# Two hybrid layers on one core: the second linear-attention pair moved behind the four softmax heads

## What is computed

```python
h = rms_norm(x, norm_g[l]) * (1.0 + scale) + shift
gq, gk, gv, glr, gz, dq, dk, dv, dz = split_columns(h @ w_in[l])
gq, gk, gv = split(silu(causal_depthwise_conv(concat(gq, gk, gv), conv_w[l])))
# gla, 4 heads: log_a = log_sigmoid(glr @ w_gk + b_gk) / 16, b = cumsum over chunks of 64
# k_dec = k * exp(b_end - b); state = exp(b_end) * state + k_dec^T v; o = q @ state
# o = rms_norm(o, g_out) * silu(z)
# diff, 4 heads: q, k rms-normed, p = softmax of the masked scores of two halves,
# o = rms_norm((p0 - lam * p1) @ v, g_out) * (1 - lam_init) * silu(z)
x = x + gate * (concat(o_gla, o_diff) @ w_out[l])
```

## Time and profile before

| | |
|---|---|
| median of 3 runs | 1952.38 us (1950.65 to 1952.73) |
| the profiled execution's own time | 1950.45 us |
| its span, first to last instruction | 1948.6 us |
| TensorE busy | 1849.8 us, 95% of the span |
| VectorE, ScalarE, GpSimd busy | 1017.4, 879.6, 876.4 us |
| layers of the second model | about 1361 to 1658 us and 1658 to 1948 us |

### The profile page before, as it was taken

The page is one execution under the profiler, slowest core; times in us unless marked ns, Lnnn a source line. Parts: engine busy times, 40 slices in busy tenths (PEclk is TensorE's granted clock), DMA queues, the critical chain, the costliest instruction groups (busy, mean ns, idle before and its releaser), DMA issues.

```text
span 1948.6 us, 26470 instructions
## 1 busy us (share of the span) xinstructions
PE 1849.8 (95%) x8630; PEld 1448.3 (74%) x8630; DVE 1017.4 (52%) x1675; ACT 879.6 (45%) x1371; POOL 876.4 (45%) x1064
## 2 busy tenths in 40 slices
PE   7999989999999999999899999999899989899988
PEld 5666657887888788888788787888677757676756
DVE  5667646611653468677566315623534454634451
ACT  6667644411432355555444213423445544535551
POOL 3322245655666334434236656765443325443323
PEclk9999999999999999999899999999999999999999
DMA  4121115433443221212145324523222112222212
GB/s 153 55 66 54 54 55 162 162 97 108 162 140 97 87 76 55 65 54 66 33 136 173 117 93 151 166 93 97 67 74 66 65 44 76 69 83 63 68 44 76
DMA packets 49659, 176.37 MB, mean 91 GB/s; under 512 B 5648, under 2 KB 5776, under 8 KB 49568
## 3 DMA queue, kind: packets, MB, share of 16 engines
q1 hardware_dynamic: 42368, 148.99, 24.2%
q10 hardware_dynamic: 7200, 26.22, 4.0%
HBM read 173.08 MB, written 2.10 MB: 90 GB/s over the span
## 4 chain that ended last, share of the span: by engine, by line
PE 79%; DVE 8%; ACT 7%; issue 4%; POOL 1%; DMA 0%; DVEq 0%; ACTq 0%; SPq 0%; POOLq 0%
PE ps_g L236 22%; PE ps_g L240 21%; PE ps_g L243 21%; PE ps_zt L938 2%; PE ps_s L1501 1%; PE ps_o L966 1%; PE ps_zt L1556 1%; ACT w_hi L208 1%; PE ps_o L494 1%; PE ps_o L1571 1%; PE ps_zt L484 1%; ACT scr L393 1%; PE ps_s L385 1%; DVE scr L1124 1%; PE ps_zt L476 1%
## 5 line engine op out<-in xcount | busy, mean ns | idle before, releaser
L216 POOL TENSOR_TENSOR w_lo<-raw,w_hi 128x256 fp32r<-128x256 f32 x936 | 764.7, 847 | 880.1 <-ACT w_hi L208 879.4
L208 ACT ACTIVATE w_hi<-raw 128x1024 fp32r<-128x1024 f32 x274 | 288.9, 1054 | 375.5 <-PE ps_g L243 361.6
L236 PE MATMUL ps_g<-h_hi,w_hi 128*128 128x512 f32 x1240 | 349.7, 412 | 22.2 <-ACT h_hi L270 8.5
L240 PE MATMUL ps_g<-h_lo,w_hi 128*128 128x512 f32 x1240 | 326.3, 393 | 1.0 <-DVE h_lo L275 1.0
L243 PE MATMUL ps_g<-h_hi,w_lo 128*128 128x512 f32 x1240 | 323.3, 391 | 0.3 <-DVE w_lo L224 0.3
L236 PEld LDWEIGHTS ps_g<-h_hi,w_hi 128*128 128x128 f32 x1240 | 225.6, 190 | 91.5 <-issue 39.8
L240 PEld LDWEIGHTS ps_g<-h_lo,w_hi 128*128 128x128 f32 x1240 | 234.9, 189 | 53.8 <-DVE h_lo L275 2.3
L243 PEld LDWEIGHTS ps_g<-h_hi,w_lo 128*128 128x128 f32 x1240 | 234.0, 189 | 50.9 <-DVE w_lo L224 0.7
L236 PE MATMUL ps_g<-a_hi,w_hi 128*128 128x512 f32 x920 | 249.3, 405 | 18.2 <-DVE scr L1730 4.5
L240 PE MATMUL ps_g<-a_lo,w_hi 128*128 128x512 f32 x920 | 238.5, 394 | 0.0
L243 PE MATMUL ps_g<-a_hi,w_lo 128*128 128x512 f32 x920 | 237.3, 392 | 0.0
(11 more groups left out here) (197 smaller groups left out, 2056.6 us busy)
## 6 DMA issues: line engine op xcount, KB each, us to landing
raw<-weights SPq DMA_DIRECT2D x274, 512.0 KB, 3.5
scr<-ada_weights ACTq DMA_DIRECT2D x48, 512.0 KB, 4.3
x<-x_tiles SPq DMA_DIRECT2D x8, 256.0 KB, 5.4
y<-x SPq DMA_DIRECT2D x8, 256.0 KB, 3.2
scr<-csil_dram ACTq DMA_DIRECT2D x2, 512.0 KB, 5.5
lvmask<-level_masks SPq DMA_DIRECT2D x1, 512.0 KB, 8.5
mats<-squares SPq DMA_DIRECT2D x1, 448.0 KB, 6.6
vecs<-vectors SPq DMA_DIRECT2D x1, 95.5 KB, 2.0
```

What stands on the lines that cost most here:

```text
L208: nc.scalar.activation(w_hi[:, t.rep % 2], raw[:, raw_slot(t)], ACT.Copy).then_inc(whi_ready, 1)
L216: ins = nc.gpsimd.tensor_tensor(w_lo[:, t.rep % 2, ks], raw[:, raw_slot(t), ks], w_hi[:, t.rep % 2, ks].bitcast(F32), ALU.subtract)
L236: nc.tensor.matmul(bank[:], w_hi[:, t.rep % 2, kk], rhs(k)[0], start=(first and n == 0), stop=False)
L240: nc.tensor.matmul(bank[:], w_hi[:, t.rep % 2, kk], rhs(k)[1], start=False, stop=False)
```

## The change

Two things, in both layers. **The gates' order**: `gate 0`, `gate 1` go ahead of the first half of tile 4, and what follows from them (`gate2`, `decay`, the silu table, `silu 0`) comes one or two half tiles earlier. **The items' order**: g0, d0, d1, d2, d3, g1. The second pair's six tiles are now numbers 23 to 28. Its convolutions start while d3's softmax is still going on, and its six silus come in three stretches, each between two loads of tables (two more loads a stretch). The drain holds g1's `read` and two `stat` steps in place of d3's softmax, so d3 loses its own banks and waits as the other heads do. Output row blocks are taken in the order 0, 1, 4, 5, 6, 7, 2, 3 (`BLOCK`), as their heads finish. `dec_b`, `ktok_b`, `vtok_b` get a buffer for each pair.

```diff
-B2_COLUMNS = [GLA_Z, GLA_Z + P, GLA_R]
...
+B2_COLUMNS = [GLA_Z, GLA_Z + P, GLA_R, GLA_Q, GLA_K, GLA_V, GLA_V + P]
 for _h in range(DIFF_HEADS):
     B2_COLUMNS += [m + P * _h for m in (DIFF_Q, DIFF_K, DIFF_V, DIFF_Z)]
+B2_COLUMNS += [GLA_Q + P, GLA_K + P, GLA_V + 2 * P, GLA_V + 3 * P, GLA_Z + 2 * P, GLA_Z + 3 * P]
...
-        ITEMS = [("gla", p) for p in range(GLA_PAIRS)] + [("diff", h) for h in range(DIFF_HEADS)]
+        ITEMS = [("gla", 0)] + [("diff", h) for h in range(DIFF_HEADS)] + [("gla", 1)]
...
+        OWN["gla1"] = {2 * c + 1: [("taps", c)] for c in range(4)}
+        OWN["gla1"][5][:0] = [("functions", SILU), ("silu", 0), ("silu", 1), ("functions", EXP_LN)]
+        OWN["gla1"][8] = [("functions", SILU), ("silu", 2), ("silu", 3), ("functions", EXP_LN)]
+        OWN["gla1"][10] = [("functions", SILU), ("silu", 4)]
+        OWN["gla1"][11] = [("silu", 5), ("functions", EXP_LN)]
+        for _i, _s in ((2, "decay"), (6, "decay2")):
+            OWN["gla1"].setdefault(_i, []).append((_s,))
+        for _i, _t in ((7, "k"), (9, 0), (10, 1)):
+            OWN["gla1"].setdefault(_i, []).append(("turn", _t))
+        OWN["gla1"][11].append(("update",))
...
+        DRAIN = [("split",), ("out", 0, 0, 6), ("read", G1), ("square", 0, G1), ("out", 1, 0, 2), ("stat", 0, G1),
+                 ("square", 1, G1), ("out", 1, 2, 6), ("olo", 0, G1), ("stat", 1, G1), ("out", 0, 6, 7), ("out", 1, 6, 7),
+                 ("olo", 1, G1)]
...
-                        due[2] += [("gate", p) for p in range(GLA_PAIRS)]
-                        due[3].append(("gate2", 0))
-                        due[4] += [("gate2", 1), ("decay", it)]
-                        due[5].insert(0, ("functions", SILU))
+                        due[1] += [("gate", p) for p in range(GLA_PAIRS)]
+                        due[2] += [("gate2", 0), ("gate2", 1)]
+                        due[3] += [("decay", it), ("functions", SILU, it), ("silu", 0, it)]
                         due[7].append(("decay2", it))
...
+        BLOCK = [0, 1, 4, 5, 6, 7, 2, 3]
```

More of the change, by code:

```diff
@@ L225, in split_lo_dve, with gemm @@
                                     ALU.subtract).then_inc(wlo_ready, 1)
-        def gemm(pe, t, o, rhs, kts, first, last, waits=None, free=None):
+        def gemm(pe, t, o, rhs, kts, first, last, waits=None, free=None, used=None):
             pe.wait_ge(whi_ready, t.of(1, 1))
@@ L244, in gemm @@
                                        stop=(last and n == len(kts) - 1))
-            if kts[-1][1] == KT - 1:
+            if kts[-1][1] == KT - 1 if used is None else used:
                 ins.then_inc(tile_used, 1)
@@ L1254, in hg_pool @@
                 if a: hg_d_pool(pool, a, l)
-        ITEMS = [("gla", p) for p in range(GLA_PAIRS)] + [("diff", h) for h in range(DIFF_HEADS)]
-        FIRST_TILE = {it: 3 + 4 * it[1] if it[0] == "gla" else 1 + 6 * GLA_PAIRS + 4 * it[1] for it in ITEMS}
+        ITEMS = [("gla", 0)] + [("diff", h) for h in range(DIFF_HEADS)] + [("gla", 1)]
+        FIRST_TILE = {("gla", 0): 3, ("gla", 1): 7 + 4 * DIFF_HEADS} | {("diff", h): 7 + 4 * h for h in range(DIFF_HEADS)}
         R_TILE = 2
@@ L1269, in build_program @@
         OWN["gla0"][3].remove(("silu", 0))
-        OWN["gla0"][5].insert(0, ("silu", 0))
         OWN["gla0"].setdefault(6, []).append(("silu", 4))
         OWN["gla0"][7].append(("silu", 5))
[L1273 to L1282, removed]
-                                   4: [("attn", 1), ("scores", 3)], 5: [("attn", 2)], 7: [("attn", 3)],
-                                   8: [("pv",), ("square", "o")], 9: [("stat", "o")], 10: [("olo", "o")]}}
@@ new lines, in build_program @@
+        OWN["gla1"][11].append(("update",))
+        BACK = {"gla": {0: [("turn", 0)], 1: [("turn", "k"), ("functions", EXP_LN)], 2: [("turn", 1)], 4: [("update",)],
+                        6: [("read",), ("square", 0)], 7: [("stat", 0), ("square", 1)], 8: [("olo", 0)], 9: [("stat", 1)],
+                        10: [("olo", 1)]},
+                "diff": {0: [("scores", 0)], 1: [("scores", 1)], 2: [("attn", 0), ("scores", 2)],
+                         4: [("attn", 1), ("scores", 3)], 5: [("attn", 2)], 7: [("attn", 3)],
+                         8: [("pv",), ("square", "o")], 9: [("stat", "o")], 10: [("olo", "o")]}}
@@ L1333, in schedule @@
                 if it is None:
-                    steps += [("split",), ("silu", 3, LAST)] + DRAIN
+                    steps += DRAIN
                 before = it
@@ L1393, in build_program @@
         N_BACK = 2 * GLA_PAIRS + DIFF_HEADS
+        BLOCK = [0, 1, 4, 5, 6, 7, 2, 3]
+        OUT_ORDER = [(b, b) for b in BLOCK]
         def out_n(it, m, l):
-            return l * N_BACK + (2 * it[1] + m if it[0] == "gla" else 2 * GLA_PAIRS + it[1])
+            return l * N_BACK + (6 * it[1] + m if it[0] == "gla" else 2 + it[1])
         def reader(tile, l):
```

103 lines of the change are left out of this document (34 added, 69 removed).

## The result

The changed kernel took 1938.87 us (median of 4 runs, 1937.0 to 1940.19) beside 1951.88 for the kernel before (4 runs, 1950.65 to 1952.73): ratio 0.9942, 95% interval 0.9929 to 0.9954. It is faster by 13.0 us; 5.0 were forecast, and the range ended at 1941.5. A later set gave 1938.10 against 1950.52 (0.9945, 0.9932 to 0.9959). The profiled execution took 1937.0 us, span 1934.9.

The account below looks back on a forecast made before the run. TensorE, busy 95% of the span, was taken as the bound, so only its waits and half clock count. -4.9 at the start and +2.4 beside d3 give -2.5 us a layer, -5.0 for two: 1947.4 us, range 1941.5 to 1954.5.

Parts of the forecast that it names:

- the start of the layer: Old waits at the pairs and their half clock go, shorter waits at tiles 5 and 6 come: -4.9 us a layer.
- The four waits of before: TensorE's waits at the pairs, 4.49, 0.64, 1.33 and 0.91 us, 7.4 us in all, would go.
- The three new waits: At tiles 5 and 6 TensorE would wait for w_lo, w_hi and w_lo: 3.5 us together (3.0 to 4.3).
- half clock behind the 4.49 us wait: Eight matmuls at 1.2 GHz from tile 7 on cost 1.6 us a layer, which would go with the wait.
- The second pair beside d3: Waits ahead of d3's third scores (5.0), then 0.5, then 4.3 us; with the drain, +2.4 us a layer (-0.5 to +5).
- the drain: End of the layer: two waits at the last statistics, 1.25 and 3.0 us, in place of five, 10.8 us in all.
- The k transpose's wait: Third wait beside d3, for VectorE's decay2 behind taps, table loads and silus: 4.3 us (3.2 to 5.3).
- Half clock behind the third wait: After the wait ahead of the k transpose the clock falls, costing 1.7 us a layer.
- (a): Gain given back: start waits lower the clock in both layers, third wait at its upper end; 1951.6 us, chance 0.29.
- (b): A switch of functions stops ScalarE for twice its row: 2.6 us more a layer, 1952.6 us, no difference; chance 0.04.
- (c): Slower: the chain to the k transpose is longer than walked; at 6 us more 1959 us; chance 0.11.
- (d): Better: first and third waits come to 4 and 3 us, clock holds at the start; 1942 us, chance 0.10.

Follow-up runs that it names:

- before_fill: The kernel before with four matmuls of 512 constant columns in the 4.49 us wait ahead of tile 7, in each layer; 1946.5 us, ratio 0.9981.
- warm1: The changed kernel with five filler matmuls ahead of d3's third scores, in each layer; 1940.9 us, ratio 0.9959 to the kernel before.
- warm2: The changed kernel with five filler matmuls ahead of d3's third scores and five more ahead of the k transpose; 1935.5 us, ratio 0.9929 to the kernel before.
- loads2: The changed kernel with one more pair of table loads ahead of the second pair's silus 0 and 1; 1946.7 us, ratio 0.9982 to the kernel before.
- gates: The kernel before with the gates' order alone, the items' order unchanged; 1943.3 us, ratio 0.9966.
- start_order: The changed kernel with the first table load and silu 0 behind the weights of tile 6; 1936.5 us, ratio 0.9933 to the kernel before.
- before_again_2: The kernel before, unchanged, profiled once more; the second model began at 1369.3 us and its first layer took 240.6 us.

## Why the prediction was wrong in size

The signs, places and releasers held; the sum was 8 us short. The step that failed is a term of it, the -4.9 for the start of the layer: the runs show -6.4, 3 us in all. The layers make up 0.5 more beside d3, the stretch behind them 1.4, and some 3 us are not resolved.

- **The start of the layer** was forecast at -4.9. The gates' order alone gained 3.0 us a layer there, and the three waits that went with the items' order (0.64, 1.33 and 0.91) come to 3.4 from start to start: -6.4, 1.5 more than the term. Three things were mis-sized. The four waits of before come to 8.0 from start to start, not 7.4 (the rows' idle leaves out some 0.16 at each). The three new waits came to 2.8, not 3.5. And they brought no half clock (0.6 allowed). That would be 1.9; where 0.4 of it went the runs don't show. The half clock behind the 4.49 us wait was priced right (1.6; before_fill shows 1.5 and 1.6). The new waits were overpriced mostly because GpSimd was quicker than in the rows that I took:

```profile
1385.56 2.81 POOL L213 TENSOR_TENSOR w_lo<-raw,w_hi 128x256 fp32r<-128x256 f32 x4 [6.94 <-ACT w_hi L205]
1388.33 1.04 POOL L1803 TENSOR_TENSOR scr<-scr 128x512 f32<-128x512 f32 x1
```

  The earlier trace rows have 3.27 and 1.40 for these.
- **The second pair beside d3**: 5.0 and then 0.5 forecast, 5.06 and none measured; the drain 1.25 and 3.0, 1.33 and 3.04. The k transpose's wait was put at 4.3 us and is 3.07 in the first layer and 2.49 in the second. But warm1 shows the wait as it is at full clock, 4.76. On d2's clock (its second scores start at 1555.00 before, d3's at 1536.72 now) the third scores start at 1563.8, where 1563.7 was forecast, and the k transpose at 1585.6, where 1586.0 was. So the walk along seven engines' pieces was right to half a microsecond, and the rest is the half clock that the prediction called free but didn't take off the wait. What is left of the layers' 4.25 us each beside the start's 6.4 is +2.15, where +2.4 was forecast.
- **Half clock behind the third wait** was priced at 1.7; filling that wait gave 1.5 and 1.6 there beside the changed kernel (warm2).
- **Behind the layers** nearly nothing was forecast; that stretch is 1.4 us shorter, with less half clock in it (1.5, 1.4 and 3.7 us in the changed kernel's profiles, 7.8 to 8.0 in before's).
- **The rest**: 8.5 and 1.4 make 9.9, and the medians differ by 12.4 to 13.0. The two 95% intervals, 9.0 to 13.9 us and 8.0 to 13.3, both hold 9.9, and the remainder is no larger than the spread that the first model's clock gives between executions. Whether it is all chance is open: two of the changed kernel's profiles and both warm ones begin at 1367.7 to 1368.0, but the third at 1372.8, and those of its other variants at 1369.1 to 1372.1.
- **The rivals**: (a) no fall at the start; (b) a load costs its row and nothing more (loads2); (c) the chain wasn't longer; (d) had the clock at the start right, and its 1942 was the nearest.

## What to carry to other kernels

A wait removed from a busy TensorE is worth its length from start to start, except where a later wait on another engine's chain takes it up. The half clock behind it (1.5 to 1.6 us here) comes on top if no later wait takes it up and the clock doesn't fall somewhere else instead, as it did in gates. Fill one wait with matmuls on constants to see which it is. After a reordering, read the longest new wait backwards and ask of each engine whether it was idle while its input lay ready: here VectorE's two operations, moved ahead of the taps, gave 2.7 and 3.0 us at their place, 3.7 over the two layers, against 8.5 for the whole change (the medians say 8.2, but the first model's clock is in them). And compare stretches between two marks of the program, not spans, where the clock falls at different places.

## What was not expected of the hardware

In unchanged code the granted clock was 1.00 in one execution and 0.50 in another over the same matmuls, which moved the second model's begin by up to 5 us. The same 2.2 us wait was followed by half clock in the first layer only (the profile of before), the second only (the changed kernel's), both (start_order) or neither (before_again_2). Three waits of 0.8 us within 8 us brought no fall.
